# One rounding of an expert weight chunk moved down ScalarE's queue, behind the up reads and the activations' roundings

## What is computed

```python
# 32 experts, each token goes to the 4 with the highest router logits
def expert_block(args):
    xblk, e = args
    gu = xblk @ w_gate_up[e] + b_gate_up[e]          # 1024 -> 2048
    g_lin = jnp.minimum(gu[:, :D_EXPERT], SWIGLU_LIMIT)
    u_lin = jnp.clip(gu[:, D_EXPERT:], -SWIGLU_LIMIT, SWIGLU_LIMIT)
    act = g_lin * jax.nn.sigmoid(SWIGLU_ALPHA * g_lin) * (u_lin + 1.0)
    return act @ w_down[e] + b_down[e]               # 1024 -> 1024
```

## Time and profile before

| | |
|---|---|
| three runs | 2076.27, 2077.97, 2084.07 us |
| profiled execution, its own time | 2080.97 us |
| profiled execution, span | 2079.2 us |
| busy over the whole span: PE, PE weight loads | 1910.5 us (92%), 1599.3 us (77%) |
| VectorE, ScalarE, GpSimd | 1570.2 us (76%), 1436.7 us (69%), 595.9 us (29%) |
| mean granted TensorE clock | 0.963 of full speed |
| the rounding L1052 in all | 384 instructions, 715.9 us |
| the subtraction L1057 in all | 384 instructions, 861.1 us |

### The profile page before, as it was taken

One profiled execution on the slowest core, in us unless ns is written; L12 is line 12 of the kernel. 1 busy time (PEld: TensorE's weight loads), 2 busy tenths in 40 slices (PEclk: granted clock), 3 DMA queues, 4 the chain that ended last, 5 costly groups with the idle time before them and its releaser, 6 DMA issues.

```text
span 2079.2 us, 61172 instructions
## 1 busy us (share of the span) xinstructions
PE 1910.5 (92%) x25003; PEld 1599.3 (77%) x25003; DVE 1570.2 (76%) x2115; ACT 1436.7 (69%) x1851; POOL 595.9 (29%) x448
## 2 busy tenths in 40 slices
PE   6999998889979779999999999999998999899897
PEld 3444873333644379999999999999998999899896
DVE  5331333778662368888998999899999999999996
ACT  4330322777564458877888888888888888888884
POOL 3222121767741231122221321232232122213221
PEclk8999999999899879999999999999999999999998
DMA  5111100000142468999999999999999999999996
GB/s 172 41 41 61 42 21 1 1 1 1 41 152 112 160 211 289 319 327 312 326 322 339 326 339 328 341 331 341 336 341 338 334 345 336 333 338 331 347 315 229
DMA packets 142377, 479.27 MB, mean 231 GB/s; under 512 B 15140, under 2 KB 30244, under 8 KB 142240
## 3 DMA queue, kind: packets, MB, share of 16 engines
q1 hardware_dynamic: 129440, 444.13, 59.5%
q0 software_dynamic: 12864, 34.09, 6.9%
HBM read 457.34 MB, written 34.87 MB: 237 GB/s over the span
## 4 chain that ended last, share of the span: by engine, by line
PE 31%; DVE 12%; issue 10%; DMA 8%; ACT 3%; DVEq 1%; POOL 0%; POOLq 0%; SPq 0%; ACTq 0%
PE banks L1772 29%; DVE region_c L1057 7%; DMA region_a<-w_down_dram 7%; DVE region_b L1599 1%; ACT region_b L1446 1%; ACT region_b L1450 1%; PE banks L1738 1%; DVE region_b L1604 1%; PE banks L1765 1%; DVE region_b L1620 1%; DVE region_b L1613 1%; PE banks L1751 1%; DVE region_b L1609 1%; DMA region_b<-rows_out,region_d 0%; ACT region_b L1434 0%
## 5 line engine op out<-in xcount | busy, mean ns | idle before, releaser
L1772 PE MATMUL banks<-region_b,region_c 128*128 128x128 f16 (+2 forms) x18432 | 1154.1, 226 | 65.6 <-DVE region_b L1620 41.2
L1772 PEld LDWEIGHTS banks<-region_b,region_c 128*128 128x128 f16 x18432 | 1136.3, 99 | 73.4 <-ACT region_b L1450 48.4
L1057 DVE TENSOR_TENSOR region_c<-region_a,region_c 128x2048 f16<-128x2048 f32 x256 | 574.1, 2283 | 4.2 <-DMA region_b<-rows_h,region_d 4.2
L1052 ACT ACTIVATE region_c<-region_a 128x2048 f16<-128x2048 f32 x256 | 478.0, 1912 | 51.9 <-PE banks L1772 26.4
L1375 POOL TENSOR_TENSOR region_d<-region_d 80x1 f32<-80x1 f32 x96 | 60.5, 630 | 945.8 <-DVE region_d L1572 636.3
L1057 DVE TENSOR_TENSOR region_c<-region_d,region_c 128x2048 f16<-128x2048 f32 x128 | 287.0, 2281 | 0.0
L1052 ACT ACTIVATE region_c<-region_d 128x2048 f16<-128x2048 f32 x128 | 237.9, 1917 | 0.0
L353 PE MATMUL banks<-region_a,region_d 128*128 128x512 f16 x960 | 208.2, 379 | 1.7 <-PEq L96 1.7
L353 PEld LDWEIGHTS banks<-region_a,region_d 128*128 128x128 f16 x960 | 93.8, 98 | 116.3 <-issue 4.3
L1459 ACT ACTIVATE region_b<-banks,region_d 80x512 f32<-80x512 f32 x128 | 80.5, 677 | 138.7 <-PE banks L1765 138.7
L1364 POOL DMA_INDIRECT region_b<-rows_h,region_d x64 | 135.8, 2122 | 44.2 <-issue 44.2
(11 more groups left out here) (301 smaller groups left out, 2197.8 us busy)
## 6 DMA issues: line engine op xcount, KB each, us to landing
region_d<-w_gate_up_dram SPq DMA_DIRECT2D x128, 1024.0 KB, 8.7
region_a<-w_gate_up_dram SPq DMA_DIRECT2D x128, 1024.0 KB, 8.1
region_a<-w_down_dram SPq DMA_DIRECT2D x128, 1024.0 KB, 8.5
region_d<-w_in_dram SPq DMA_DIRECT2D x14, 1024.0 KB, 5.0
region_b<-x_dram SPq DMA_DIRECT2D x4, 1024.0 KB, 9.5
region_b<-w_out_dram SPq DMA_DIRECT2D x8, 512.0 KB, 3.7
rows_out<-region_b SPq DMA_DIRECT2D x8, 512.0 KB, 2.6
rows_h<-region_b SPq DMA_DIRECT2D x8, 512.0 KB, 2.7
```

Source lines behind the costliest of these rows:

```text
L1052: act.activation(part_hi[r][:, 2 * q:2 * q + 2, :], raw[r][:, 2 * q:2 * q + 2, :], ACT.Copy).then_inc(s_hi9, 1)
L1057: dve.tensor_tensor(part_lo[r][:, at, :], raw[r][:, at, :], part_hi[r][:, at, :], ALU.subtract).then_inc(s_lod, 1)
L1772: mm = pe.matmul(out_ap, a, b, start=(first and s == 0), stop=(k == KT - 1 and s == 2), skip_group_check=True)
```

## The change

ScalarE's `high_part` is taken apart into `high_half`, one rounding of one half, and for chunk 5 the second half's rounding is called after the last `act_high` and not ahead of the up reads. The instructions and their number stay the same. The order in which the halves of chunks are rounded, on which the running count rests, stays the same too.

```diff
+        def high_half(act, j, uses, q):
+            r = j % RING
+            act.wait_ge(s_raw[r][q], uses * 16)
+            act.activation(part_hi[r][:, 2 * q:2 * q + 2, :], raw[r][:, 2 * q:2 * q + 2, :], ACT.Copy).then_inc(s_hi9, 1)
+
         def high_part(act, j, uses):
-            r = j % RING
             for q in range(2):
-                act.wait_ge(s_raw[r][q], uses * 16)
-                act.activation(part_hi[r][:, 2 * q:2 * q + 2, :], raw[r][:, 2 * q:2 * q + 2, :], ACT.Copy).then_inc(s_hi9, 1)
+                high_half(act, j, uses, q)
...
                     act.wait_ge(s_u, i * 16 + 8)
-                    high_part(act, 5, i * 2 + 2)
+                    high_half(act, 5, i * 2 + 2, 0)
                     for f in range(KT):
                         up_read(i, f)
                         if f in (3, 5):
...
                         x_split(i + 1, 0)
                     act_high(i, 2)
                     act_high(i, 3)
+                    high_half(act, 5, i * 2 + 2, 1)
                     if not last:
                         high_part(act, 6, i * 2 + 3)
```

## The result

The changed kernel takes 2091.09 us (median of 7 runs, 2086.18 to 2092.35), the kernel before 2076.4 us (7 runs, the three above among them, 2072.82 to 2084.07). The ratio is 1.0069, with a 95% interval of 1.0054 to 1.0084: slower by 14.7 us (0.7%), where the forecast was 2080 and no change.

A forecast was written before the change was run, and what follows sets the result against it. It took PE alone to bound the first stage and a loop through VectorE and PE the later two. Terms: 0 - 1.4 + 3.9 - (2.1 - 0.85) - 0.5 = +0.75 us; forecast 2080, range 2071 to 2088.

The forecast's parts named there:

- The item model: Expert phase: ScalarE's 1.80 us shift, less idle time, delays the gate product; periods 40.40, 41.0 and 43.4 us.
- Other takers of the moved rounding: Check of VectorE's subtractions and SyncE's loads behind the moved rounding; it ends 0.9 us ahead of chunk 5's second-half subtraction.
- None waits: Claim that VectorE's subtractions of chunks 5, 6 and 7 never wait for the shifted roundings.
- - (2.1 - 0.85) - 0.5: Item after the fifteen 128-column periods gains 2.1 us, loses 0.85 to late copies; the last item gains 0.5.
- 9.0: 128-column stage: gain in us, 602.1 measured against 593.1 for fifteen undisturbed periods of 39.54.
- part of that 3.0 may be absent from the runs' gain: Profiled execution lay 3.0 us above the runs' median; the changed kernel has no late transfer to lose by.
- the late copies: ScalarE's first three y copies (L1467) end later, so the 128-column gate product starts 0.85 us late per item.
- (a): Rival: the copies' lateness is hidden and only the clip wait goes: -14.8 us, about 2063 on the median; chance 0.07.
- (b): Rival: new idle time before the gate product halves PE's clock, 1.6 us per 128-column item: +25, 2105; chance 0.08.
- (c): Partial case: copies exposed 0.45 to 1.25 us instead of 0.85, -6 to +6 us over fifteen items; inside the range.

The follow-up runs named there:

- The late issue in the kernel before: The kernel before; in the last item only, GpSimd does four one-column additions before issuing the first scatter: 2085.89 us, ratio 1.0036.
- the signal: Changed kernel; in the last item only, VectorE's subtraction of chunk 4 waits for a GpSimd semaphore placed behind the first scatter: 2084.01 us, ratio 1.0036.
- the old order in the last item: Changed kernel, with chunk 5's second-half rounding back ahead of the up reads in the last item only: 2088.79 us.
- the version with the copies first: Changed kernel, with ScalarE's first three y copies moved ahead of the second x split: 2068.56 us, ratio 0.9954 to the kernel before.
- the doubled dose: Changed kernel, with both halves of chunk 5 rounded behind the activations' roundings in all items: 2145.83 us.

## Why the prediction was wrong

**The item model was right.** It said periods of 40.40, 41.0 and 43.4 us; measured 40.41 to 40.45, 41.05 to 41.06, and 260.02 us for the first stage as before. It said that the gate product starts 0.85 late (5.37 became 6.25 us after the down product: 0.88, of which 0.71 is idle time of PE and not 0.8 to 0.9), that VectorE's wait at L1570 grows to 1.7 (1.75), and that the 144- and 128-column stages change by -1.4 and +3.9 us in the profiled execution: -1.1 and +4.2. Up to the last item but one the sum said +2.5, the trace has 4.0, of which 0.9 arose ahead of the first item.

**The step that failed** is in "Other takers of the moved rounding", with "None waits", and in the sum's last terms, "- (2.1 - 0.85) - 0.5". I followed ScalarE's queue, VectorE, PE and SyncE, but not GpSimd, whose scatter waits for ScalarE's scaled rows and with them for PE. In the loop its issues are covered: one of 3.27 us stands in the item at 1628.85, whose period is the undisturbed 39.54. At the end nothing covers them, and the tail changed by +6.6 us and not by -1.75. Two things make up this term: PE's results reach GpSimd 0.86 us late against VectorE, and the issue is then held up and takes 6.99 us and not 1.42. The late issue in the kernel before shows the holding in the old order (5.34 us, an end of 95.2), the signal takes most of it away (3.52, 88.5), the old order in the last item leaves it (7.08, 93.6). It hangs on less than a microsecond: 0.36 to 0.54 us ahead of the subtraction in the four traces with a short issue, 0.33 and 0.34 behind it in the changed kernel. The trace of before could have warned: in its items with 128 columns GpSimd's issue took 3.27 us where it started inside a subtraction, and 1.42 in the last item.

```profile
1514.71 4.48 DVE L1057 TENSOR_TENSOR region_c<-region_d,region_c 128x2048 f16<-128x2048 f32 x2
...
1517.24 3.27 POOL L1369 DMA_INDIRECT rows_out<-region_b,region_d  x1 [0.20 <-issue]
```

**A term that was mis-sized** is the base of the gain. "9.0" us at 128 columns came from one execution whose stage took 602.1 us; the second trace of the same kernel has 596.9, so that there was 3.7 us to gain and not 9.0. Of the 9.0 us, 5.4 were clip waits and about 2.4 longer waits for `find`. Four traces with the old order have 17.8, 12.4, 11.9 and 21.4 us of clip waits, of which 7.5 in each lie in the first stage, where they cost nothing; what was there to gain is 10.3, 4.9, 4.4 and 13.9 us. The prediction saw the direction ("part of that 3.0 may be absent from the runs' gain") and allowed 1 us for it. Over the two traces of each kernel, which differ by 15.7 us, the mean change is 0 at 160 columns, -0.9 at 144, +6.9 at 128, +7.4 in the end, and +2.3 ahead of the first item, where the traces of all kernels scatter between 754.4 and 760.6. So, leaving out what lies ahead of the first item, about half of the loss is the 128-column stage (the late copies less the waits that went) and half the end. The profiled execution of before lay 4.6 us above the median of its seven runs, that of the changed kernel 0.5, so that the first two traces show only 10.6 us of the 14.7.

**The rivals.** (a), the copies hidden and only the wait gone, is not what the changed kernel does, but it is what the version with the copies first does: 2067.1 against the 2064.4 that -14.8 makes of the span. The rule of the Trainium skill beside it, to look for the gaps of the engine with the highest occupancy ("Perfetto Trace Analysis", Identifying the Most-Contended Engine, and for the gaps Optimization Strategy), points to a real gap; by itself it does not see that another engine has no room for the instruction that was moved. (b), PE's clock: granted 0.98 in the 128-column stage with the new gap, no lower than before (0.97), and no gate product is slow (5.52 us in all fifteen items). The first down product, which stands behind an idle time of 2.0 us, ran partly at the lower clock in six of the fifteen items, in the first trace of before in eleven. With the doubled dose the lower clock also comes to the second down product, behind 2.87 us of idle time. The Trainium skill's rule on back-to-back matmuls ("Perfetto Trace Analysis", Matmul Optimizations) speaks against such gaps. This case agrees for the one of 2.87 us; the idle time of 0.71 us cost nothing but itself. (c) came to 0.01 to 0.05 us an item.

**What stays open.** Why a held-up issue ends at 3.6 us in two kernels and at 7.3 to 7.4 in four is not settled. Two points of VectorE's work lie 1.3 to 1.4 us ahead of these two ends, about the time of an undisturbed issue: the start of the second half of the subtraction (2.2 after the first) and the end of the three products with the sigmoid behind it (6.0, in all ten traces). In the rows just above, too, the issue ends 1.3 us after the subtraction. So it looks as if the issue runs only when VectorE lets it in between two instructions, but nothing was run that tells which of VectorE's instructions hold it up, or why it is let in at 2.2 in two kernels only. Where the scatter of a few us ahead of the first item comes from was not tried.

## What to carry to other kernels

An instruction moved down a full queue shifts all that follows by its issue distance less the idle time on the way; follow the shift on every queue to the first waiter that can't absorb it, and ask what else frees room there, as the three copies did here for 1.17 us. Look at the last item by itself: what the loop hides is bare there, and an engine that waits for nothing in it can overtake another. Price a wait that hangs on transfers from more than one execution, for a single trace had 17.8 us where the next had 12.4.

## What the runs showed of the hardware

In the last item of ten traces, GpSimd's issue of an indirect DMA of 80 rows takes 1.42 us when it starts 0.36 to 0.54 us ahead of a VectorE subtraction of 128x2048 (two of them, 4.48 us together) and 2.95 to 7.08 us when it starts after the first has begun. The subtraction takes 4.48 or 4.49 us either way. A semaphore that GpSimd's program counts up behind such an issue reached VectorE before the issue had run: VectorE was let go 0.06 us ahead of the issue's start in the trace and 3.58 ahead of its end, so that a signal of this kind does not order the two engines.
